# Filler products before the norms, and norm sums and a, b products dealt out, on TensorE

## The reference

```python
def gdn_mixer(h, w_in, conv_w, A_log, dt_bias, out_norm, w_out):
    proj = h @ w_in
    qkv, gate, a, b = jnp.split(proj, [n_qkv, n_qkv + H * dv, n_qkv + H * dv + H], axis=-1)
    qkv = jax.nn.silu(causal_depthwise_conv_2(qkv, conv_w))
    q, k, v = jnp.split(qkv, [H * dk, 2 * H * dk], axis=-1)
    q = l2norm(q.reshape(B, S, H, dk))
    k = l2norm(k.reshape(B, S, H, dk))
    beta = jax.nn.sigmoid(b.astype(jnp.float32))
    g = -jnp.exp(A_log) * jax.nn.softplus(a + dt_bias)
    o = gated_delta_rule_chunked(q, k, v, g, beta)
    o = rmsnorm(o, out_norm) * jax.nn.silu(gate.reshape(B, S, H, dv))
    return o.reshape(B, S, H * dv) @ w_out
```

## Time and profile before

| What | Value |
|---|---|
| Median of three runs | 3508.07 us |
| The profiled execution's own time | 3508.96 us |
| Its span, first to last instruction | 3507.0 us |
| PE busy | 3282.8 us (94%) |
| DVE busy | 1928.8 us (55%) |
| ACT busy | 1562.3 us (45%) |
| DMA, mean of the core | 153 GB/s |
| Mean granted TensorE clock | 0.959 of full speed |

### The profile page before, as it was taken

The page is one execution under the profiler, slowest core; times in us unless marked ns, Lnnn a source line. Parts: engine busy times, 40 slices in busy tenths (PEclk is TensorE's granted clock), DMA queues, the critical chain, the costliest instruction groups (busy, mean ns, idle before and its releaser), DMA issues.

```text
span 3507.0 us, 48865 instructions
## 1 busy us (share of the span) xinstructions
PE 3282.8 (94%) x19206; PEld 2817.0 (80%) x19206; DVE 1928.8 (55%) x2159; ACT 1562.3 (45%) x1825; POOL 136.5 (4%) x151
## 2 busy tenths in 40 slices
PE   8987799899899999989999999999769999998899
PEld 6886787788778888978888888888657888898787
DVE  4456655655554546655455554555665555484554
ACT  4447344444544445434444444444335444463443
POOL 0000000100000003120000000000000000003000
PEclk9998899899999999899999999999979999998999
DMA  6542355355255555405555545565411655652164
GB/s 210 191 121 82 95 191 179 126 182 190 79 186 188 172 183 171 128 14 168 189 182 180 178 155 187 171 196 191 150 49 49 193 178 192 187 159 78 53 194 138
DMA packets 423766, 535.41 MB, mean 153 GB/s; under 512 B 21122, under 2 KB 370798, under 8 KB 423632
## 3 DMA queue, kind: packets, MB, share of 16 engines
q1 hardware_dynamic: 421840, 528.76, 47.3%
q0 software_dynamic: 1792, 4.72, 0.6%
HBM read 532.36 MB, written 1.05 MB: 152 GB/s over the span
## 4 chain that ended last, share of the span: by engine, by line
PE 90%; DVE 6%; ACT 3%; issue 1%; DMA 0%; SPq 0%; ACTq 0%; DVEq 0%
PE banks L133 23%; PE banks L135 23%; PE banks L134 23%; PE banks L130 3%; PE banks L131 3%; PE banks L132 3%; PE banks L312 2%; PE banks L1666 2%; PE banks L247 1%; DVE w_lo L114 1%; ACT w_hi L106 1%; PE banks L1616 1%; PE banks L1123 1%; PE banks L1111 1%; ACT xT_hi L191 0%
## 5 line engine op out<-in xcount | busy, mean ns | idle before, releaser
L114 DVE TENSOR_TENSOR w_lo<-raw,w_hi 128x2048 fp32r<-128x2048 f32 x514 | 1176.3, 2294 | 664.6 <-ACT w_hi L106 664.6
L106 ACT ACTIVATE w_hi<-raw 128x2048 fp32r<-128x2048 f32 x514 | 982.0, 1915 | 599.6 <-PE banks L135 494.0
L133 PE MATMUL banks<-w_hi,xT_hi 128*128 128x512 f32 (+3 forms) x2736 | 1054.7, 385 | 76.9 <-issue 33.2
L135 PE MATMUL banks<-w_hi,xT_lo 128*128 128x512 f32 (+3 forms) x2736 | 1040.1, 380 | 0.0
L134 PE MATMUL banks<-w_lo,xT_hi 128*128 128x512 f32 (+3 forms) x2736 | 1039.0, 380 | 0.0
L133 PEld LDWEIGHTS banks<-w_hi,xT_hi 128*128 128x128 f32 x2736 | 524.7, 192 | 173.7 <-issue 39.0
L135 PEld LDWEIGHTS banks<-w_hi,xT_lo 128*128 128x128 f32 x2736 | 523.8, 191 | 96.5
L134 PEld LDWEIGHTS banks<-w_lo,xT_hi 128*128 128x128 f32 x2736 | 524.9, 192 | 90.8
L133 PE MATMUL banks<-w_hi,hidT_hi 128*128 128x512 f32 x1056 | 411.9, 390 | 0.0
L135 PE MATMUL banks<-w_hi,hidT_lo 128*128 128x512 f32 x1056 | 411.1, 389 | 0.0
L134 PE MATMUL banks<-w_lo,hidT_hi 128*128 128x512 f32 x1056 | 410.9, 389 | 0.0
(11 more groups left out here) (407 smaller groups left out, 2411.0 us busy)
## 6 DMA issues: line engine op xcount, KB each, us to landing
raw<-ffn_w_gate_up SPq DMA_DIRECT2D x352, 512.0 KB
raw<-ffn_w_down SPq DMA_DIRECT2D x264, 512.0 KB
raw<-ffn_w_gate SPq DMA_DIRECT2D x88, 512.0 KB
raw<-ffn_w_up SPq DMA_DIRECT2D x88, 512.0 KB
raw<-gdn_w_in SPq DMA_DIRECT2D x64, 512.0 KB
raw<-sc_w_in SPq DMA_DIRECT2D x24, 512.0 KB
raw<-rg_w_in SPq DMA_DIRECT2D x32, 336.0 KB
raw<-nsa_w_in SPq DMA_DIRECT2D x20, 512.0 KB
```

The costliest lines, as they stand in the source:

```text
L106: c.nc.scalar.activation(c.w_hi[r][:], c.raw[r][:], ACT.Copy).then_inc(c.sem("w_hi_split"), 1)
L114: c.nc.vector.tensor_tensor(c.w_lo[r][:], c.raw[r][:], c.w_hi[r][:].bitcast(F32), ALU.subtract).then_inc(c.sem("w_lo_split"), 1)
L133: mm(out, x_hi, w_hi, start=start, stop=False)
L135: return mm(out, x_lo, w_hi, start=False, stop=stop)
```

## The change

There are three parts. The first is in `pe_norm`: in front of a stage's transposes PE now issues filler products, matmuls of a constant 128x384 bf16 tile into a bank of the norm, whose result the transposes overwrite. 28 of them stand where the source stage has an output norm, 14 where it has none and the stage is a mixer, none in front of the other FFNs. The second: the norm sums leave `beside_gate(0)` and stand in four portions of 8 products behind the q, k, v steps 8 to 11; ACT takes the square root in front of the a and b step's split and not behind gate step 0. The third: the step for a and b is no longer one of its own on PE. A new argument `between` of `pe_project` puts three of its small matmuls ahead of each three of gate step 0; `slab_used` for the slab of a and b is counted behind the last of them. The instruction lists of DVE, POOL and SP stay as they were.

```diff
--- before.py
+++ after.py
@@ -233,11 +233,17 @@
         dve_rstd(c, dve, st)
 
 
+BUSY_MATMULS = 14
+
+
 def pe_norm(c, pe, st):
     n = st.norm
     if n == 0:
         pe.wait_ge(c.sem("masks_made"), MASK_STEPS)
     src = c.h if st.kind == "ffn" else c.xn
+    if n and (st.kind != "ffn" or st.source.post is not None):
+        for _ in range(BUSY_MATMULS if st.source.post is None else 2 * BUSY_MATMULS):
+            c.nc.tensor.matmul(c.bank[NORM_BANKS[1]][:, 0:3 * P], c.ident_bf[:], c.causal_bf[:], start=True, stop=True)
     for m, t in PARTS:
         if st.kind == "ffn":
             wait_for_h(c, pe, st, m, t)
@@ -580,7 +586,7 @@
     step_loop(c.nc.sync, pr, one)
 
 
-def pe_project(c, pe, pr, after=None, ready=None, norm=None):
+def pe_project(c, pe, pr, after=None, ready=None, norm=None, between=None):
 
 
     if norm is not None and (pr.loop or pr.two_banks):
@@ -624,6 +630,8 @@
                 x = slice(lo, hi)
                 w = slice(base + tile * pr.width // 2, base + (tile + 1) * pr.width // 2)
                 out = c.bank[bank][0:pr.width // 2, tile * (hi - lo):(tile + 1) * (hi - lo)]
+            if between is not None:
+                between(s, tile, k)
             last = pe_matmul3(c, out, c.xT_hi[0:pr.rows, k, x], c.xT_lo[0:pr.rows, k, x],
                               c.w_hi[r][0:pr.rows, w], c.w_lo[r][0:pr.rows, w], first, end, pr.form == "feat")
             if tile == tiles - 1 and k % kd == kd - 1:
@@ -1609,13 +1617,6 @@
         return last
 
     def beside_gate(s):
-        if s == 0:
-            pe.wait_ge(c.sem("gdn_squares"), 8 * (u + 1))
-            for t in range(TOKS):
-                for n in range(16):
-                    last = mm(c.bank[3][:, t * 16 + n:t * 16 + n + 1], v.sq[:, n, t * P:(t + 1) * P], c.ones[:, 0:1],
-                              start=True, stop=True)
-            last.then_inc(c.sem("gdn_norms"), 1)
         if s == 1:
             pe.wait_ge(c.sem("gdn_g_ready"), u + 1)
             pe.wait_ge(c.sem("gdn_root"), u + 1)
@@ -1641,9 +1642,34 @@
                                       start=True, stop=True)
                 last.then_inc(c.sem("gdn_gc_spread"), 1)
 
-    pe_project(c, pe, qkv, norm=st.norm)
-    pe_project(c, pe, ab)
-    pe_project(c, pe, gate, after=beside_gate)
+    def beside_qkv(s):
+
+        if s < 8:
+            return
+        pe.wait_ge(c.sem("gdn_squares"), 8 * u + 2 * (s - 8) + 2)
+        for t in range(TOKS):
+            for n in range(4 * (s - 8), 4 * (s - 7)):
+                last = mm(c.bank[3][:, t * 16 + n:t * 16 + n + 1], v.sq[:, n, t * P:(t + 1) * P], c.ones[:, 0:1],
+                          start=True, stop=True)
+        if s == qkv.steps - 1:
+            last.then_inc(c.sem("gdn_norms"), 1)
+
+    def between_gate(s, t, k):
+
+        if s:
+            return
+        n, r, _ = slab_number(ab.slab, 0)
+        if t == 0 and k == 0:
+            pe.wait_ge(c.sem("w_lo_split"), n + 1)
+        x, w = slice(t * P, (t + 1) * P), slice(k * ab.width, (k + 1) * ab.width)
+        last = pe_matmul3(c, c.bank[ab.step % 3][:, t * ab.width:(t + 1) * ab.width], c.xT_hi[:, k, x], c.xT_lo[:, k, x],
+                          c.w_hi[r][:, w], c.w_lo[r][:, w], k == 0, k == KD - 1)
+        if t == TOKS - 1 and k == KD - 1:
+            last.then_inc(c.sem("slab_used"), 1)
+
+    pe_project(c, pe, qkv, norm=st.norm, after=beside_qkv)
+    pe.wait_ge(c.sem("projection_read"), ab.step - 2)
+    pe_project(c, pe, gate, after=beside_gate, between=between_gate)
     pe.wait_ge(c.sem("gdn_tokens_read"), 2 * u + 2)
     for b in range(2):
         for t in range(TOKS):
@@ -1764,6 +1790,8 @@
                               ).then_inc(c.sem("gdn_squares"), 1)
 
     act_project(c, act, qkv, act_first_tap(c, v.cv, v.taps, G_TAPS - 1), after=activated)
+    act.wait_ge(c.sem("gdn_norms"), u + 1)
+    scalar.activation(flat(v.norm), c.bank[3][:, 0:32], ACT.Sqrt, bias=v.eps).then_inc(c.sem("gdn_root"), 1)
     act_project(c, act, ab)
 
     scalar.activation(v.a_log, v.a_log, ACT.Exp).then_inc(c.sem("gdn_exp_a"), 1)
@@ -1771,9 +1799,6 @@
     scalar.activation(v.beta, v.ab[:, :, G_HEADS:2 * G_HEADS], ACT.Sigmoid).then_inc(c.sem("gdn_beta"), 1)
 
     def beside_gate(s):
-        if s == 0:
-            act.wait_ge(c.sem("gdn_norms"), u + 1)
-            scalar.activation(flat(v.norm), c.bank[3][:, 0:32], ACT.Sqrt, bias=v.eps).then_inc(c.sem("gdn_root"), 1)
         if s == 1:
             act.wait_ge(c.sem("gdn_tokens"), 2 * u + 1)
             for d in range(2):
```

## The result

The changed kernel takes 3531.3 us (median of 4 runs, 3524.1 to 3531.7) where the kernel before takes 3508.2 us (3506.8 to 3508.5): 0.6% slower, ratio 1.0064, 95% interval 1.0052 to 1.0077. The prediction of 3508 us, range 3497 to 3515, was wrong. The profiled execution is 3531.53 us long, with a span of 3529.8 us: 22.8 us more than before.

The account below looks back on a forecast made before the run. The prediction took PE, with 90% of the chain of waits, to bound the kernel, time being won where PE waits or runs slowly. Fillers -2.4 and delta-rule stages +2.1 gave -0.3 us, rounded to none: 3508 us, range 3497 to 3515.

Parts of the forecast that it names:

- so I take full clock here: Delta-rule stages: norm sums inside the last q, k, v steps take 7.0 us; gate step 0 with a and b 11.1.
- Rival 3: Delta-rule stages: dealing out does not save the clock; half of gate step 0 slow gives +11, 3519 us; chance 0.09.
- 0.5 in gate step 0: Delta-rule stages: a clock of 0.5 in gate step 0, named beforehand as a sign of being wrong.
- The chain to g: Delta-rule stages: 13.85 us from the last product for a and b to g, so PE stands for 7.7 us.
- The price of the idle wait: Behind PE's wait for g: PE resumes at half clock and loses 2.1 us per delta-rule stage, bounds 1.7 to 5.8.
- Part 1: Filler products ahead of the stages' transposes: -2.4 us in sum.
- The FFN behind kv: No wait for the norm there: 28 fillers take 6.9 us, then 13.78 instead of 15.00; +5.7, bounds +3.3 to +7.9.
- the recurrent mixer: Start of that stage: fillers in its 7.39 us wait, 2.8 us left idle; -3 us, bounds 0 and -4.1.
- sparse attention, put at 0: Start of sparse attention: it waits again for its operand behind its transposes, so fillers gain 0.
- rivals, 1: Gate step 0: small products hide behind large ones, about 5.8 us instead of 11.1; -8, so 3500 us; chance 0.14.
- 2 by the waits: Delta-rule stages: PE does not wait for g, both stages win their clock; 3487 us; chance 0.05.
- Rival 4: Fillers do better: FFN behind kv costs only 3.3, or clock rises early; -4 to -8, 3501 to 3504 us; chance 0.12.

## Why the prediction was wrong

**The failed step** is "so I take full clock here". The prediction took it from 40 us of attention at 1.00 and applied it to two things: norm sums between large products, where it held in all stages, and gate step 0 with a and b behind the last sums, where it did not. Instead of 11.1 us the step took 20 us in both stages, 9 us more each. The row could not carry it: the trace has no matmul of under 65 columns in those 40 us, against 1 and 16 here. The comparison of versions gives the size: with the sums one step earlier the stages cost +2.7 and +2.7 us against before, in the changed kernel +10.1 and +12.7, so 17.5 of the 22.8 us are this step and what follows from it. Rival 3 named the mechanism and decided at a third of the step's work slow, but priced half of it slow, 3519 us; all of it was. Its chance of 0.09 was too low, and the evidence for more stood in the rows: a and b alone begin at 0.98 and the clock then falls, so it was known that small products end at half clock, and the attention row said nothing on what stands ahead of such a mix. What moved the clock was the pair, sums and then the mix; the sums ahead of large products, and the mix behind them, kept 1.00. The prediction had itself named 0.5 in gate step 0 as a sign of being wrong.

**The chain to g** was right. The prediction summed 13.85 us from the last product for a and b to g. In the changed kernel PE's running sums start at 1472.44, 13.83 us behind that product (the next one starts at 1458.61), and PE stood still for 5.33 and 6.46 us instead of 7.7, shorter only because gate step 1 began at half clock too. Where the dealt step was at full clock the wait was 7.47 us. ACT's rows, which answer to the earlier trace rows, are the ones foreseen, with the next split started at once:

```profile
1458.86 1.91 ACT L106 ACTIVATE w_hi<-raw 128x2048 fp32r<-128x2048 f32 x1 [15.31 <-PE banks L135]
...
1464.94 0.22 ACT L1799 ACTIVATE silu<-silu 128x16 f32<-128x16 f32 x1
1465.07 1.90 ACT L106 ACTIVATE w_hi<-raw 128x2048 fp32r<-128x2048 f32 x1
```

**The price of the idle wait** was 2.1 us per stage in the prediction, bounds 1.7 to 5.8. By the windows the stretch lost 3.8 and 4.2 us in the changed kernel (22.17 and 22.51 to the end of gate step 3, against 18.34 before). Of that 2.3 and 2.7 us lie up to the end of gate step 2, behind the wait: the transposes take 3.3 us instead of 1.7. So the price itself was about right. The other 1.5 us are gate step 3, 7.4 instead of 5.95, which the experiments show without a wait too.

**Part 1** was right in its sum, and partly by luck. The -2.4 us compare with -2.3 measured. The FFN behind kv: predicted 6.9 us of fillers and +5.7; the changed kernel has 7.4 us and 15.00 turned into 13.37, so +5.8, and leaving the fillers out gained 5.2 us at that place. FFN behind the recurrent mixer: -1.65 and -1.5. But the recurrent mixer, -3 predicted, is -3.1 in the changed kernel and -0.1 with the fillers alone, the same code and the same 2.8 us left idle. Its start won 2.1 and 1.9 us (12.09 and 12.27 instead of 14.15); the rest of the stage won 1.0 in one and lost 1.8 in the other. With the fillers alone the missing 3 us are made up elsewhere: kv with its FFN costs only 4.3 us, and sparse attention, put at 0, gives 1.2.

**Unforeseen**: +2.7 us in sparse attention, which the change touches only at its start. The window of its step of 48 columns, kernel before:

```profile
2520.28:2532.72 12.44, 5.43 (x49) 5.32 (x47) 10.67 (x16) 5.11 (x3) 0.00 (x0) 0.72 0.66 215
```

And the changed kernel (the stage also starts 1.1 us slower: its first 64 matmuls take 18.80 us where they took 17.71):

```profile
2528.70:2543.10 14.40, 7.39 (x50) 7.26 (x48) 10.76 (x16) 5.11 (x3) 0.00 (x0) 0.61 0.58 190
```

The same instructions take 2 us more at a lower clock. It appears with norm sums or a and b moved (+2.3 and +2.0 us when each is moved alone) and not with fillers alone (-1.2). But with sized fillers it is absent although a and b are moved (-1.3), or both (-1.4). So it doesn't follow from the moved work; that it goes with how the stage happens to meet the drops of the clock is likely and not shown. The range had allowed a microsecond either way for such stretches.

Of the rivals, 1 is excluded by the spacing (11.1 us at full clock, not 5.8) and 2 by the waits. Rival 4's lower price behind kv, +3.3, did not occur in the changed kernel (+5.8).

## What to carry to other kernels

Before small products are dealt among large ones, look at what PE does directly ahead. Behind dense work the mix stayed at full clock in ten of ten stages; behind one-column products the clock fell at its start in five of six and stayed down for the rest of it, nearly twice the time of the step. A clock read off another stage, with wider products, was no warrant for this one. And when small work is moved out of a stretch, follow who inherits both the half clock and the cover that it gave to a chain on ACT and DVE; here dealing out the one part, the other, or both with the wait filled ended within noise of dealing out nothing, while bf16 fillers in waits that PE had anyway gave 0.2 to 0.3%, as long as each group stood in a real wait. A term of 1 to 3 us per stage can match in one trace and miss in the next, so it is to be checked in more than one kernel.

## What the runs showed of the hardware

- PE busy in every part of a window is no sign of full clock. The same 96 matmuls, half of 16 and half of 256 columns, took 11.1 us at 1.00 and about 20 us at 0.51, with PE and its weight loads both busy throughout. The Trainium skill ("TensorE: Matmul & The Clock Gate", Part 1) says that the throttled state is the default and that activity releases it. This trace does not agree for such a mix: it stayed at half clock from 0.4 us on to the end of the 20 us, with no gap between its matmuls, and the measurement decides. The clock came back 4.9 and 2.3 us into the large products behind it.
- At full clock such a group of three small and three large products takes 0.25 + 0.44 us, at half clock 0.49 + 0.79; the spacing of the small ones goes from 0.11 to 0.21 us, and their weight loads take 0.33 us each instead of 0.19, so the loads slow down with the clock as well.
- 28 fillers of 384 columns took 4.41 us at full clock, 0.158 us each, and 7.4 us behind kv, where the clock was 0.61.
- Small products alone can lose the clock too: the 48 products of 48 columns in sparse attention, entered from products of 512 columns at 1.00, stayed at 1.00 in the kernel before and fell to half 3 us into the step in the changed kernel, with the same instructions (5.4 and 7.4 us).
